# Projection, two normalizations and feed-forward of a layer in one stage, by token thirds

## What is computed

```python
def _layer_norm(x, g, b):
    xc = xf - jnp.mean(xf, -1, keepdims=True)
    var = jnp.mean(xc * xc, -1, keepdims=True)
    return (xc * lax.rsqrt(var + LN_EPS) * g + b)

y = jnp.concatenate([o_a, o_b], -1) @ w_out
x = _layer_norm(ALPHA * x + y, g1, b1)
ff = (jax.nn.silu(x @ w1) * (x @ w3)) @ w2
x = _layer_norm(ALPHA * x + ff, g2, b2)
```

## Time and profile before

| | us |
|---|---|
| median of 3 runs | 3558.7 (3558.47 to 3560.22) |
| profiled execution | 3561.3 |
| its span, first to last instruction | 3559.7 |
| PE busy | 3117.9 (88%) |
| PEld busy | 2790.9 (78%) |
| DVE busy | 1626.1 (46%) |
| ACT busy | 797.7 (22%) |
| mean granted TensorE clock | 0.908 |

### The profile page before, as it was taken

How to read it: one execution, slowest core, us unless ns; L and a number is a source line. 1 busy time by engine, 2 the same in 40 slices (tenths; PEclk the granted TensorE clock), 3 DMA queues, 4 the chain that set the end, 5 groups by cost and what they waited for, 6 DMA issues and landing times. The chain is left out here.

```text
span 3559.7 us, 49762 instructions
## 1 busy us (share of the span) xinstructions
PE 3117.9 (88%) x19939; PEld 2790.9 (78%) x19939; DVE 1626.1 (46%) x3131; ACT 797.7 (22%) x1551; POOL 248.1 (7%) x279
## 2 busy tenths in 40 slices
PE   8997799969879999999997968155897999999997
PEld 8997566548859999999986955033495999999995
DVE  2112287656444443344344245988335343344335
ACT  2110276523131000000003113454404000000002
POOL 2001000023000000000002720011100000000000
PEclk9999899977889999999998985567898999999998
DMA  6222310131202011111102330000111111001101
GB/s 232 99 86 102 110 38 1 42 123 31 68 12 83 36 49 36 60 36 36 48 1 75 118 105 0 0 1 15 45 36 36 60 48 60 36 36 48 59 13 49
DMA packets 63277, 193.46 MB, mean 54 GB/s; under 512 B 7812, under 2 KB 32292, under 8 KB 53792
## 3 DMA queue, kind: packets, MB, share of 16 engines
q1 hardware_dynamic: 58176, 172.86, 13.8%
q0 software_dynamic: 3904, 12.46, 1.1%
q10 hardware_dynamic: 1008, 5.41, 0.4%
HBM read 159.68 MB, written 35.36 MB: 55 GB/s over the span
## 5 line engine op out<-in xcount | busy, mean ns | idle before, releaser
L163 PE MATMUL f_up<-f_x_high,f_w_high 128*128 128x352 f32 x2112 | 686.3, 325 | 62.6 <-DVE f_x_low L638 48.5
L165 PE MATMUL f_up<-f_x_high,f_w_low 128*128 128x352 f32 x2112 | 681.5, 323 | 0.0
L164 PE MATMUL f_up<-f_x_low,f_w_high 128*128 128x352 f32 x2112 | 681.4, 323 | 0.0
L163 PEld LDWEIGHTS f_up<-f_x_high,f_w_high 128*128 128x128 f32 x2112 | 399.8, 189 | 65.5 <-issue 65.5
L164 PEld LDWEIGHTS f_up<-f_x_low,f_w_high 128*128 128x128 f32 x2112 | 400.4, 190 | 0.0
L165 PEld LDWEIGHTS f_up<-f_x_high,f_w_low 128*128 128x128 f32 x2112 | 400.0, 189 | 0.0
L163 PE MATMUL f_down<-f_h_high,f_w_high 128*128 128x352 f32 x1056 | 344.9, 327 | 14.0 <-DVE f_w_low L157 8.2
L602 DVE TENSOR_TENSOR f_gated<-f_silu,f_up 128x352 f32<-128x352 f32 x132 | 68.8, 521 | 614.5 <-PE f_up L165 590.7
L616 DVE TENSOR_TENSOR xT_sb<-xT_sb,f_down 128x352 f32<-128x352 f32 x480 | 248.5, 521 | 208.1 <-PE f_down L165 208.1
L164 PE MATMUL f_down<-f_h_low,f_w_high 128*128 128x352 f32 x1056 | 342.0, 324 | 0.0
L165 PE MATMUL f_down<-f_h_high,f_w_low 128*128 128x352 f32 x1056 | 341.5, 323 | 0.0
(11 more groups left out here) (429 smaller groups left out, 5034.6 us busy)
## 6 DMA issues: line engine op xcount, KB each, us to landing
f_raw<-w SPq DMA_DIRECT2D x66, 1024.0 KB, 4.8
pe<-pe_y SPq DMA_DIRECT2D x27, 528.0 KB, 2.9
pe_raw<-w_in_e SPq DMA_DIRECT2D x27, 512.0 KB, 3.9
po<-po_y SPq DMA_DIRECT2D x14, 528.0 KB, 2.9
po_raw<-w_in_o SPq DMA_DIRECT2D x14, 512.0 KB, 4.2
xT_sb<-xT ACTq DMA_DIRECT2D x4, 1056.0 KB, 11.3
ro_x<-po SPq DMA_DIRECT2D x8, 528.0 KB, 3.7
y<-xT_sb SPq DMA_DIRECT2D x3, 1408.0 KB, 5.2
```

The costliest lines, as they stand in the source:

```text
L163: pe.matmul(out, wh, xh, start=n == 0, stop=False)
L164: pe.matmul(out, wh, xl, start=False, stop=False)
L165: return pe.matmul(out, wl, xh, start=False, stop=n == depth - 1)
```

## The change

One new function, `project_and_feed`, takes the place of `dense` for the projection, of both `normalize` stages and of `feed_forward`. It is one stage, called for each layer after `free_semaphores` (which stood behind the projection before).

- The projection's outer loop runs over the thirds, the inner one over the 8 output tiles, with all its split weights kept on the chip (`out_w_high`, `out_w_low`) and written out instead of looped. Its 24 groups alternate between the two banks of `down`. ScalarE makes the high part of weights and input, VectorE the low part; a third is split as a whole (2816 columns). The low part of `oT` is written in the place of `oT`.
- The mean and the variance of a third no longer take 8 matmuls each. VectorE adds the 8 tiles up first (`tree`: 1408, 704 and 352 columns, L708), and one matmul each does the rest. These are placed between the groups of the next third's projection; those of the last third stand in the first feed-forward groups.
- The first two hidden tiles are made in the order `FIRST` (tile, third): (0,0) (0,1) (1,0) (1,1) (0,2) (1,2), so that the last third of the normalized input is wanted last. Their weights are loaded behind the projection's weights.
- The steps 1 to 9 are as before.
- In the last step the down products of steps 9 and 10 are one: thirds outside, 24 groups of 12 matmuls. The down weights of step 10 are split into the room of the first up weights, between the two last hidden tiles. The adding-up, mean and variance of the second normalization stand between the groups of the next third.
- The store of `y`, in layer 2, still goes third by third behind its gain and bias.

The core of the diff, TensorE's list and parts of VectorE's:

```diff
-                for c in range(NCH):
-                    for kt in range(KT):
-                        mm = pe.matmul(mean[:, c, 0:CH], k.mean_w[:], k.xT[:, kt, c * CH:(c + 1) * CH],
-                                       start=kt == 0, stop=kt == KT - 1)
-                    mm.then_inc(mean_of, 1)
...
+                def mean(j):
+                    pe.wait_ge(summed, j + 1)
+                    pe.matmul(stats(j)[0], k.mean_w[:], sums[:], start=True, stop=True).then_inc(mean_of, 1)
...
+                for c in range(NCH):
+                    for m in range(KT):
+                        n = c * KT + m
+                        if c == 0:
+                            pe.wait_ge(wo_split, m + 1)
+                        if m == 0:
+                            pe.wait_ge(xo_split, c + 1)
+                        if n >= 2:
+                            pe.wait_ge(o_added, n - 1)
+                        multiply(pe, down[:, n % 2, 0:CH], lambda q: (wo[0][:, m, q], wo[1][:, m, q]),
+                                 lambda q: (X_high(q, c), X_low(q, c)), KT).then_inc(o_product, 1)
+                        if c and m == 1:
+                            mean(c - 1)
+                        if c and m == 4:
+                            variance(c - 1)
...
+                for s, (f, c) in enumerate(FIRST):
+                    pe.wait_ge(w13_split, f + 1)
+                    pe.wait_ge(x_split, c + 1)
+                    if s >= NCH:
+                        pe.wait_ge(h_split, s - NCH + 1)
+                    half(f, c, s % NCH, 0, gate)
+                    if s == 0:
+                        pe.wait_ge(o_added, outs)
+                        mean(NCH - 1)
+                    half(f, c, s % NCH, 1, value)
+                    if s == 1:
+                        variance(NCH - 1)
...
+                pe.wait_ge(w2_split, LAST + 1)
+                pe.wait_ge(h_split, PAIRS * 2 * NCH)
+                for c in range(NCH):
+                    for m in range(KT):
+                        n = c * KT + m
+                        pe.wait_ge(added, (LAST - 1) * outs + n - 1)
+                        multiply(pe, down[:, n % 2, 0:CH], lambda f: weights(f, m), lambda f: hidden(f, c), 4).then_inc(product, 1)
+                        if c and m == 2:
+                            mean(NCH + c - 1)
+                    if c:
+                        variance(NCH + c - 1)
+                mean(2 * NCH - 1)
+                variance(2 * NCH - 1)
...
+                def tree(src, part, out_, sem, total):
+
+                    half = [(part[:, 0:4], src[:, 0:4], src[:, 4:8]), (part[:, 0:2], part[:, 0:2], part[:, 2:4]),
+                            (out_, part[:, 0], part[:, 1])]
...
-        normalize(nc, k, "n0", 0)
-        feed_forward(nc, k, "f0", d["w13_0"], d["w2_0"])
-        normalize(nc, k, "n1", 1)
...
+        project_and_feed(nc, k, "f0", k.oT, d["w_out_e"], 0, d["w13_0"], d["w2_0"])
```

More of the change, by code:

```diff
@@ new lines, in _ @@
+                split_out(0)
+                out_high(0)
+                out_high(1)
+                split_out(1)
+                out_high(2)
+                split_out(2)
+                for m in range(3, KT):
+                    out_high(m)
+                square(0)
+                first_high(0)
+                deviation(0)
+                affine(0)
+                split_in(0)
+                square(1)
+                act.wait_ge(squares_up, 2)
+                first_high(1)
+                deviation(1)
@@ L582, in step @@
                             act.wait_ge(product, (i - 1) * outs)
-                        act.activation(H.high[:, slot, n // NCH, cols(c)], G[:, n % 2], ACT.Copy).then_inc(h_high, 1)
-                pipeline(act, step)
+                        act.activation(h[0][:, slot, n // NCH, cols(c)], G[:, n % 2], ACT.Copy).then_inc(h_high, 1)
+                middle(act, step)
+                step(act, LAST, 0)
+                for c in range(NCH):
+                    square(NCH + c)
+                    deviation(NCH + c)
+                    affine(NCH + c)
@@ L635, in _ @@
-                split13(0, 0, used=False)
-                for n in range(KT):
-                    dve.wait_ge(x_high, n + 1)
-                    dve.tensor_tensor(out=X.low[:, n], in0=k.xT[:, n], in1=X.high[:, n].bitcast(F32),
-                                      op=ALU.subtract).then_inc(x_split, 1)
-                split13(0, 1, used=False)
-                pipeline(dve, step)
-                add(PAIRS - 1)
+                    steady(i, slot, 0)
+                    split13(2 * i + 2, 0, (2 * i + 1) * NCH)
@@ new lines, in step @@
+                    steady(i, slot, 1)
+                    add(i - 1, first=isinstance(i, int) and i == 1)
+                    split13(2 * i + 3, 1, (2 * i + 2) * NCH)
+                    split2(i)
+                middle(dve, step)
+                steady(LAST, 0, 0)
+                dve.wait_ge(w2_loaded, PAIRS * 16)
+                dve.wait_ge(value, (2 * LAST + 1) * NCH)
+                split_on(dve, w2_high, PAIRS, w2_split, raw2[:], first13[:, 0], first13[:, 1])
+                steady(LAST, 0, 1)
@@ new lines, in add_last @@
+                def add_last(c, ms):
+                    for m in ms:
+                        n = c * KT + m
+                        dve.wait_ge(product, (LAST - 1) * outs + n + 1)
+                        xm = k.xT[:, m, cols(c)]
+                        dve.tensor_tensor(out=xm, in0=xm, in1=down[:, n % 2, 0:CH], op=ALU.add).then_inc(added, 1)
+                add_last(0, range(KT))
+                sum_up(NCH)
+                for c in range(1, NCH):
+                    j = NCH + c - 1
+                    add_last(c, [0])
+                    if c == 2:
+                        invert(j - 1)
+                        add_last(c, [1])
+                        scale(j - 1)
+                        add_last(c, [2])
+                    else:
+                        add_last(c, [1, 2])
+                    centre(j)
+                    add_last(c, [3, 4, 5])
+                    sum_squares(j)
+                    add_last(c, [6, 7])
+                    sum_up(j + 1)
```

409 lines of the change are left out of this document (270 added, 139 removed).

## The result

| | before | changed |
|---|---|---|
| median, us | 3559.46 (4 runs, 3558.47 to 3570.55) | 3479.16 (4 runs, 3476.51 to 3481.71) |
| profiled execution; its span, us | 3561.3; 3559.7 | 3479.08; 3477.4 |
| mean granted TensorE clock | 0.908 | 0.907 |

The changed kernel takes 0.976 of the time of before (95% interval 0.974 to 0.978). It gained 80.3 us where 116.2 were forecast; 3479 lies outside the range of 3424 to 3462. What is to be explained is 34 us: the profiled execution took 3479.1, the sum said 3445.1.

The account below looks back on a forecast made before the run. TensorE's product stream was taken to bound projection and feed-forward, a serial chain the gap between. Front 94.3 plus tail 21.9 gave 116.2 us off 3561.3, 3445.1; with the median 2.6 lower, 3443 us, range 3424 to 3462.

Parts of the forecast that it names:

- The bound and its end: Projection and feed-forward bound by TensorE's products, the gap between by serial steps; afterwards no stretch over 8 us without products.
- Front: Stage start to sixth gated tile, by overlapping normalization with products: 157.6 and 156.9 us, gains 47.7 and 46.6.
- the wait for third 2: Ahead of the feed-forward's fifth pair TensorE waits 3.3 us for the last third's input, plus 2.0 us at half clock.
- Rival (b): Weight supply binds in the projection: later tiles each 1.0 to 1.4 us late, 9.5 us a layer, 3462; chance 0.09.
- Tail: Last gated tile to end of second normalization: 86.2 us a layer, gains 10.9 and 11.0.
- (c): Clock falls in the tail's down products with alternating banks: 38 us more a layer, 3520; chance 0.05.
- (d): Clock falls over all merged parts, front and tail, making it slower than before: 310 us more, 3750; chance 0.03.
- the wait of the last hidden tile: At the tail's start, the last hidden tile is 1.6 us late; nothing added for a clock fall.
- between the sixth and the last tile the change leaves the loop as it is: From sixth to last gated tile of each layer no time changes, so the sum needs only front and tail.
- if the loop's period of before changes: Listed sign in the feed-forward loop that would show the forecast wrong; no size given.
- Rival (a): Five unexplained waits where the loop turns back vanish: 14.1 us, up to 8 us of half clock, 3421; chance 0.09.
- the side case of (a): At the loop's turns, the sixth wait, missing in the kernel before, appears too: 3447.

Follow-up runs that it names:

- e4_eps128: Changed kernel with the 4-byte tile eps widened to 128 bytes, so x and all weight tiles start on multiples of 128 bytes: 3458.2 us.
- e11_all32: Changed kernel with eps at 128 bytes and a 32-byte unused tile ahead of the attention output; every tile of the stage 32 bytes behind a multiple of 128: 3448 us.
- e9_finer: e6 with finer steps: third 2 readied in halves in front, last third's centring, squaring and scaling reordered in the tail: 3403.0 us.
- e8_rel32: Changed kernel with eps at 128 bytes and 32 unused bytes ahead of x's high part; weights 0 from the high, 32 from the low part: 3463 us.
- e5: Changed kernel with eps widened to 96 bytes; x on multiples of 128, weights 96 bytes behind one: 3457.0 us.
- e6: e4_eps128 with the feed-forward's loop written out on every engine, so nothing jumps back: 3432.0 us.
- e7: e4_eps128 with the tail of the kernel before put back (separate last down products, second normalization as its own stage): 3466.1 us.
- e2: Kernel before with 32-byte unused tiles ahead of the up weights and behind the down weights; weights 96 bytes from x: 3573.7 us.
- e12: Kernel before with 32 unused bytes ahead of its up and down weights and 96 behind; weights 32 bytes from x: 3592.6 us.
- e1: Changed kernel with eps widened to 64 bytes, nothing else; weights 64 bytes from x: 3459.4 us.
- e3: Changed kernel with eps at 64 bytes and a 32-byte unused tile ahead of x's high part; weights 64 and 96 from high and low part: 3453.3 us.
- e10: Kernel before with its feed-forward loop written out on every engine: 3552.0 us.

## Right and wrong, point by point

**The bound and its end: right.** Between the first projection product and the last down product TensorE never stands longer than 3.6 us, and that at a turn of the loop; the 24 us for which it stood ahead of the first up product of each layer are gone.

**Front: the mechanism right, sizes near.** The sum had 149.4 and 148.7 from P to 6. With all distances 0 it is 147.9 and 147.1 (e4_eps128), with full clock behind the wait for third 2, for which the sum had 2.0 us; with half clock there it is 151.5 (layer 1 of e11_all32). The wait for third 2 was 2.9 us (3.3 forecast); behind it 23 products in 5 us at a clock of 0.70 where 31 would pass at full, 8 x 0.16 = 1.3 us (2.0 forecast); the variance's wait of 0.9 did not show. Two steps of the sum there are slightly off as added: 17.0 less 15.9 is 1.1 and not 0.9, and the steps behind it come to 36.2 and not 36.0; by the timeline the input was there some 35.7 us after the last product (1059.69 against 1024.0). Rival (b) did not come: no product of the projection waited for a weight beyond the first.

**Tail: right, step by step.** 86.0 for 86.2, and the marks between agree too: square of the third before at 50.8 (forecast 51.0), sum for the last mean at 57.9 (58.2), last square at 70.5 (70.9). TensorE waited twice for 1.2 us in the last third (1.6 forecast). Over the down products the clock stays full, so rivals (c) and (d) did not come:

```profile
1772.00:1826.00 54.00, 49.79 (x296) 47.11 (x296) 35.32 (x41) 11.79 (x13) 0.00 (x0) 1.00 0.00 1
```

The 0.82 of the whole tail comes from the chain behind them, where TensorE has only a mean and a variance left and runs at half clock. That nothing had to be added for the wait of the last hidden tile was partly luck: behind the same 1.8 us the clock fell in e4_eps128, e11_all32 and e9_finer in layer 1 and in e8_rel32 in layer 2.

**The step that failed: "between the sixth and the last tile the change leaves the loop as it is".** Its instructions are the same, its operands' places and its turns were not. The forecast priced a product matmul at 0.159 us by rows of the kernel before, for all 3168 up products a layer and 576 of the projection; in the changed kernel they took 0.1622 in the up products and 0.1628 in the projection. For the loop that is 60 pairs x 0.15 = 9.0 us a layer, in front 576 x 3.8 ns + 6 x 0.15 = 3.1: 24 us in all. By the stretches of changed less e4_eps128 it is 24.5, but the agreement is partly luck: of the 3.9 and 4.0 us in front some 1.6 each is the clock behind the wait for third 2, the slower pairs ahead of that wait are hidden by it, and the turns' waits and clock differ by a few us between the two executions. The distance itself is some 21 to 23 of the 24.5. This is the larger part of the 34, and no row of before could have shown it; the allocation shows where it comes from: a 4-byte tile ahead of all weights. The forecast's own sign came, "if the loop's period of before changes": 7.63 became 7.78.

**Rival (a) had the right object and the wrong sign.** The turns' waits did not vanish but became six of six: the loop of e4_eps128, with before's pitch, is as long as before's in layer 1 and 6.8 us longer in layer 2, where it has the one turn more. What came is the side case of (a), that the sixth turn appears, priced at 4 us (3447 against 3443). The forecast had no case of it together with something else.

**The mixers: taken as unchanged, and they are, but not to the microsecond.** In the changed kernel TensorE waited 5.2 us for a weight of the first dense stage, behind a DMA that VectorE waited for; TensorE's and VectorE's waits from 0 to 345 us:

```profile
DVE pe_w_high L155 <- DMA pe_raw<-w_in_e: 29.8, 3, 24.0
...
PE pe_acc L163 <- DVE pe_w_low L157: 5.2, 1, 5.2
```

The same wait stands in the profiled executions of e5, e6, e7, e2 (5.2 to 5.8 us) and e12 (2.1), and not in before, e1, e3, e4, e8, e9, e10 and e11, on kernels of both kinds. So it is no work of the change; what brings the DMA late was not tried. It accounts for the larger part of the 5.3 us, not surely for all: the sum puts the first projection product at 920.6, the six kernels with the changed front and without this wait have it at 916.8 to 923.4 (mean 920.4), the four with it at 921.4 to 926.3 (mean 924.0). The means also bear out the forecast's 1.4 us for the longer lead and the barrier. The 1.5 us in the second mixer are within what that stretch varies by.

The account closes: 24.5 for changed less e4_eps128 (the distance, with some us of clock), 6.6 for the turns (683.4 + 684.3 against 683.5 + 677.5), 6.8 ahead of the stages, less 3.1 for the two fronts of e4_eps128, 0.4 for the tails and 0.4 behind the last affine, make 34.0 of 34.0. Only the sum is that exact; each part is uncertain by 2 or 3 us.

## What to carry over

When a diff adds or reorders tiles, write down where each operand of the product stream starts, modulo 128 bytes, before taking a matmul's time from the old trace; padding the small tile cost nothing here and was worth some 20 us. A loop of this size costs about 4.5 us a turn on TensorE, so a handful of turns may be written out. And a large gain is best confirmed by stretches between marks in the trace: differences below 10 us drown in the scatter of parts that the change does not touch.

## Not expected of the hardware

- Up products of 352 columns follow each other, between the sixth and the last tile, by 159.1 to 159.3 ns on average when the weights start at the same place modulo 128 bytes as the streamed operand (both on a multiple, or both 32 behind one), by 160.0 to 160.2 at distances of 64 and 96, and by 162.2 at 32. The down products at a distance of 32 (e12) take 161.4.
- A turn of a loop of some 860 products costs 2.4 to 3.6 us of waiting and mostly some 4.5 us in all (3.8 for each of the two waits in layer 2 of before); the same loop written out costs nothing instead. The wait came at six of six turns in the changed kernel and its six variants with the same list of instructions, at five of six in before, e12 and e7, and at four in e2. Before, e2 and e12 have one list of instructions, so what decides it is not the list alone; every turn with a wait has a packet of the instruction queue at its start, and the five turns without have none near them.
- Behind waits of about 3 us at turns and for third 2, and behind the 1.8 us of the last hidden tile, the granted clock fell to half in some executions and stayed full in others of the same list of instructions (151.5 against 147.9 us from P to 6, 87.8 against 86.0 in the tail).
